# MoE routed in one level: experts ranked directly, slots gathered from the tokens, results added to x every turn, 18 ring slots in place of 16

## The reference, cut to what matters

```python
def hier_moe(h, w_rg, w_re, w_gate, w_up, w_down):
    pg_logits = h @ w_rg                       # 4 groups
    g_sel = argmax(pg_logits); p_sel = softmax(pg_logits)[g_sel]
    le_sel = (h @ w_re).reshape(..., 4, 8)[g_sel]   # the 8 experts of that group
    top_v, top_i = top_k(le_sel, 2)
    weights = p_sel * softmax(top_v)           # two experts per token
    expert_idx = g_sel * 8 + top_i             # of 32 experts
    act = silu(h @ w_gate[e]) * (h @ w_up[e]) * weights   # 1024 -> 256
    return act @ w_down[e]                     # 256 -> 1024, summed over the two experts
```

## Time and profile before

| | us |
|---|---|
| median of 3 runs (lowest to highest) | 1233.63 (1232.28 to 1236.47) |
| span of the profiled execution | 1228.4 |
| PE busy in the span | 1094.6 (89%) |
| DVE / ACT busy | 387.7 (32%) / 240.3 (20%) |
| moved by DMA | 298.75 MB, mean 243 GB/s |

### The profile page before, as it was taken

How to read it: one execution, slowest core, us unless ns; L and a number is a source line. 1 busy time by engine, 2 the same in 40 slices (tenths; PEclk the granted TensorE clock), 3 DMA queues, 4 the chain that set the end, 5 groups by cost and what they waited for, 6 DMA issues and landing times.

```text
span 1228.4 us, 15895 instructions
## 1 busy us (share of the span) xinstructions
PE 1094.6 (89%) x6152; PEld 601.8 (49%) x6152; DVE 387.7 (32%) x992; ACT 240.3 (20%) x494; POOL 86.3 (7%) x189
## 2 busy tenths in 40 slices
PE   8999988677799999998898799999999999879776
PEld 7776667364789446352333334444444634223232
DVE  2623354233683436211232120134001621123213
ACT  2320134232400113111111031131101311111102
POOL 6333130130000000000000000000000000000000
PEclk9999999898796999889989899999999998998889
DMA  9650374782700256699999994425423569999993
GB/s 296 175 174 12 99 246 134 205 338 87 267 1 1 77 154 257 283 421 421 421 421 420 419 305 152 132 78 205 146 103 138 239 249 421 423 421 420 420 420 123
DMA packets 87712, 298.75 MB, mean 243 GB/s; under 512 B 16067, under 2 KB 52475, under 8 KB 57902
## 3 DMA queue, kind: packets, MB, share of 16 engines
q1 hardware_dynamic: 73172, 273.92, 57.9%
q0 software_dynamic: 5152, 17.05, 4.6%
q10 hardware_dynamic: 9306, 6.67, 1.8%
HBM read 292.46 MB, written 5.16 MB: 242 GB/s over the span
## 4 chain that ended last, share of the span: by engine, by line
PE 76%; DMA 9%; DVE 7%; issue 3%; ACT 3%; SPq 2%; ACTq 0%; DVEq 0%
PE ps L1205 10%; PE ps L1395 9%; PE ps L760 9%; DMA arena<-in_moe_w_up 8%; PE ps L1161 5%; PE ps L1485 5%; PE ps L1232 3%; PE ps L711 3%; PE ps L720 2%; PE ps L1242 2%; PE ps L925 1%; PE ps L1388 1%; PE ps L1283 1%; PE ps L1012 1%; PE ps L991 1%
## 5 line engine op out<-in xcount | busy, mean ns | idle before, releaser
L1205 PE MATMUL ps<-arena,hT 128*32 128x512 f32 x1024 | 131.7, 658 | 23.0 <-DMA arena<-in_moe_w_up 22.4
L760 PE MATMUL ps<-hT,arena 128*128 128x288 f32 x448 | 114.1, 417 | 0.0
L1395 PE MATMUL ps<-arena,hT 128*128 128x512 f32 x256 | 112.7, 601 | 0.0
L760 PEld LDWEIGHTS ps<-hT,arena 128*128 128x128 f32 x448 | 86.5, 195 | 26.8 <-issue 1.7
L1205 PEld LDWEIGHTS ps<-arena,hT 128*32 128x32 f32 x1024 | 35.3, 119 | 106.5 <-issue 106.5
L1395 PEld LDWEIGHTS ps<-arena,hT 128*128 128x128 f32 x256 | 48.9, 192 | 60.8 <-issue 60.8
L1232 PE MATMUL ps<-arena 128*32 128x512 f32 x512 | 58.2, 595 | 3.2 <-ACT arena L1751 3.2
L1161 PE MATMUL ps<-htok,arena 128*128 128x512 f32 (+1 forms) x96 | 60.6, 765 | 0.0
L1485 PE MATMUL ps<-arena 128*128 128x512 f32 x128 | 59.2, 605 | 0.0
L2356 DVE TENSOR_TENSOR arena<-ps,lfp 128x256 f32<-128x256 f32 x16 | 6.8, 424 | 159.5 <-ACT lfp L1746 159.5
L711 PE MATMUL ps<-cum,ident 128*128 128x256 f32 x156 | 43.7, 439 | 11.8 <-issue 11.8
(11 more groups left out here) (473 smaller groups left out, 1446.1 us busy)
## 6 DMA issues: line engine op xcount, KB each, us to landing
arena<-in_moe_w_gate SPq DMA_DIRECT2D x66, 1024.0 KB, 14.5
arena<-in_moe_w_up SPq DMA_DIRECT2D x66, 1024.0 KB, 16.5
arena<-in_moe_w_down SPq DMA_DIRECT2D x66, 1024.0 KB, 21.7
arena<-in_cache_k SPq DMA_DIRECT2D x64, 256.0 KB, 3.2
arena<-in_cache_v POOLq DMA_DIRECT2D x64, 256.0 KB, 3.6
arena<-in_w_in_odd SPq DMA_DIRECT2D x16, 1024.0 KB, 10.5
arena<-in_w_in_even SPq DMA_DIRECT2D x14, 1024.0 KB, 9.3
arena<-in_w_out_odd SPq DMA_DIRECT2D x8, 1024.0 KB, 7.1
```

The lines of the kernel that those rows point to most:

```text
L760: last = mm(ps[:, c % 4, 0:T], w[:, k, P * (c % 2):P * (c % 2 + 1)], hT[:, k, :], start=k == 0, stop=k == KD - 1)
L1205: last = mm(ps[EC * j:EC * (j + 1), q % 2, :], xgT[:, k, GC * p + EC * j:GC * p + EC * (j + 1)], ring[:, sl:sl + 2, DE * k:DE * (k + 1)], ...
L1395: last = mm(ps[:, bank, :], hT[:, k, P * i:P * (i + 1)], ring[:, oslot(2 * n):oslot(2 * n) + 2, QC * k:QC * (k + 1)], start=k == 0, stop=k ...
```

## The change

The routing has one level. DVE finds both experts of a token, PE ranks all tokens per expert in one go (`ut`, `one` and a row `esr` that adds 512 times the expert's number, minus 1) and counts them. A token's place is thus one number, `sp1` or `sp2`. For every turn q, `places` compares `code` (the places of the turn's 128 slots) with `spq1`, `spq2` and gives `pl`, tokens x slots, and `gather` takes the 128 columns of slots straight from the token rows `htok` (8 steps k, three products of 128 columns each). `spread` copies `sp1`, `sp2`, `w1`, `w2` once per layer across all partitions (`spb`), from which `places_back` makes `pwT`, the weighted way back. `out_rows` adds a turn's results to x in every turn, one turn late. `pmg`, `hgt`, `ygs`, `group_sum`, `group_in`, `group_meta` and `group_rows` are gone. PSUM banks 5, 6, 7 serve gather and `out_rows` by turns, bank 2 the transposes. The spins before the first turn are 14 and 7 instead of 8, 4, 6 and 5. The ring has 18 slots; layer 1's mixer starts loading its first six units after the last `gate_up`, two more after the last `down` (before: four after the last but one `down`, four after the last). The overflow flag, the number of the hot expert and the rounds keep their meaning.

```diff
-ROUNDS = (TP + TS) // CH
-NPR = EG // QE
-NQ = NG * NPR
-PC = 4 * NG + 1
+ROUNDS = (TP + TS) // EC
+NQ = NE // QE
+PC = 2 * NQ + 1
-MSLOTS, RSLOTS = 3 * QE, 16
+MSLOTS, RSLOTS = 3 * QE, 18
-        arena = sb("arena", [P, SLOTS * UNIT + 23700])
+        arena = sb("arena", [P, RSLOTS * UNIT + 5240])
...
-                sp.wait_ge(s.dn_ps, past(0, r, NQ, NQ - (r == 0)))
-                for j in range(4):
+                sp.wait_ge(s.gu_ps, past(0, r, NQ, NQ))
+                for j in range(6):
                     odd_load(j)
                 sp.wait_ge(s.dn_ps, past(0, r, NQ, NQ))
-                for j in range(4, SLOTS):
+                for j in range(6, SLOTS):
...
-                spin(0, 8)
-                pe.wait_ge(s.rt_oh, 2 * layer + 1)
...
+                spin(0, 14)
+                pe.wait_ge(s.rt_oh, layer + 1)
+                for i in range(3):
+                    rk = ps[:, 4, NE * i:NE * (i + 1)]
+                    for j in range(i + 1):
+                        mm(rk, (ut if j == i else one)[0:n_, :], ohs[0:n_, j, :], start=j == 0, stop=False)
+                    mm(rk, one[0:1, :], esr[0:1, :], start=False, stop=True)
...
+                spin(0, 7)
+                    def gather(q, ks):
+                        for k in ks:
+                            if k == 0:
+                                W(s.p_rdy, NQ, q + 1)
+                                if q >= 2:
+                                    W(s.xadd, 5 * NQ, 5 * (q - 1))
+                                if first and q == 0:
+                                    pe.wait_ge(s.h_ready, rows_no(n) + 3)
+                            if k >= 3:
+                                W((s.xgd, s.xga)[(k - 3) % 2], 4 * NQ, 4 * q + (k - 3) // 2 + 1)
                             for i, (r0, m) in enumerate(TOK):
+                                last = mm(ps[:, row_bank(k), 0:P], htok[0:m, i, P * k:P * (k + 1)], pl[0:m, i, :],
                                           start=i == 0, stop=i == 2)
+                    def spread():
+                        pe.wait_ge(s.meta_rdy, layer + 1)
+                        for a, src in enumerate((sp1, sp2, w1, w2)):
+                            for i, (r0, m) in enumerate(TOK):
+                                last = mm(ps[:, (5, 6, 7, 2)[a], r0:r0 + m], bc(src[0:m, i, :], [m, P]), ident[0:m, 0:m],
+                                          start=True, stop=True)
+                            last.then_inc(s.spb_ps, 1)
+                        pe.wait_ge(s.spb_act, 2 * layer + 2)
+                        pe.wait_ge(s.spb_dve, 2 * layer + 2)
+                    def out_rows(q):
+                        W(s.y_ev, 2 * NQ, 2 * q + 2)
+                        W(s.pw_rdy, NQ, q + 1)
+                        if q:
+                            W(s.xadd, 5 * NQ, 5 * q)
                         for qr in range(4):
+                            last = mm(ps[TS * qr:TS * (qr + 1), row_bank(0), 0:QC], pwT[:, q % 2, TP:T],
+                                      ysb[:, QC * qr:QC * (qr + 1)], start=True, stop=True)
+                        for j in range(1, 5):
+                            if j >= 3:
+                                W(s.xadd, 5 * NQ, 5 * q + j - 2)
+                            mm(ps[:, row_bank(j), :], pwT[:, q % 2, P * i:P * (i + 1)], ysb[:, 512 * hf:512 * (hf + 1)],
+                               start=True, stop=True).then_inc(s.o_ps, 1)
...
                             gate_up(q, range(KD))
-                            group_sum(q - 1)
+                            out_rows(q - 1)
+                        elif first:
+                            spread()
                         act_turn(q)
-                        if p == 0 and g + 1 < NG:
-                            group_in(g + 1)
-                            group_rows(g + 1)
-                        if p == 1 and g + 1 < NG:
-                            slots_in(g + 1)
+                        if q + 1 < NQ:
+                            gather(q + 1, range(KD))
                         down(q)
-                        if p == 1 and 1 <= g < NG - 1:
-                            group_out(g - 1)
...
+                    def places(q):
+                        if q:
+                            W(s.g_ps, KD * NQ, KD * q)
+                        for i in range(3):
+                            last = V.tensor_scalar(pl[:, i, :], code[:, :], spq1[:, i, q:q + 1], None, ALU.is_equal)
...
+                    def places_back(q):
+                        V.scalar_tensor_tensor(pwT[:, q % 2, :], spb[:, 0, :], pcode[:, q:q + 1], spb[:, 2, :],
+                                               ALU.is_equal, ALU.mult)
...
+                        if q + 1 < NQ:
+                            places(q + 1)
+                        places_back(q)
                         W(s.silu, NQ, q + 1)
                         V.tensor_tensor(av[:, q % 2], ps[:, q % 2, DE:2 * DE], sg[:, q % 2], ALU.mult)
+                        if q:
+                            rows_out(q - 1)
+                        if q + 1 < NQ:
+                            rows_in(q + 1)
...
+                        places(0)
                         if first:
+                            weights()
+                        rows_in(0)
+                        if first:
+                            slots_of_turns()
...
+                            overflow()
```

More of the change, by code:

```diff
@@ L1171, in group_rows @@
[L1171 to L1188 removed]
+                            last.then_inc(s.g_ps, 1)
@@ L1234, in down @@
                         last.then_inc(s.dn_ps, 1)
-                    def group_sum(q):
-                        g, p = q // NPR, q % NPR
+                    def out_rows(q):
                         W(s.y_ev, 2 * NQ, 2 * q + 2)
-                        if p == 0 and g:
-                            W(s.yg_ev, 2 * NG, 2 * g)
-                        for hf in range(2):
-                            last = mm(ps[:, 5 + hf, :], pmwT[:, g % 2, p, :], ysb[:, 512 * hf:512 * (hf + 1)],
-                                      start=p == 0, stop=p == NPR - 1)
-                        last.then_inc(s.s1_ps, 1)
@@ L1356, in round_ @@
                         turn(NQ - 1)
-                        group_sum(NQ - 1)
-                        group_out(NG - 1)
+                        out_rows(NQ - 1)
                 round_(0, "turns")
```

524 lines of the change are left out of this document (180 added, 344 removed).

## The result

The changed kernel took 1251.58 us (median of 4 runs, 1247.99 to 1252.5), the kernel before 1235.05 us beside it (1232.28 to 1241.27): a ratio of 1.0135, 95% interval 1.0097 to 1.0173. Forecast were 1215 us and a range of 1202 to 1229. The sign was wrong, and the miss is 36.6 us.

A forecast was written before the change was run, and what follows sets the result against it. The prediction took each MoE layer as DMA-bound once its loads resume. Per layer -10.8 + 2.1 - 0.9 = -9.6 us, twice, plus 0.6, made -18.6: span 1209.8, launch 1215 us, range 1202 to 1229.

The forecast's parts named there:

- Step 1: Opening, up to the end of `gate_up` of turn 0: ends 11.2 us earlier, bounds 7 and 12.
- Step 2: Ring positions 16 and 17 load in the DMA hole, leaving 5.0 us less of loads after the resumption.
- Step 3: Turn 0 behind its `gate_up`: activation after 10.1 us, `down` done after 22.3, DMA standing still for 2.2.
- Steps 4 and 5: Turns 1 to 6: plain turn 21.4 us, another DMA stop of 3.2, `gate_up` 6 starts 170.8 after the resumption.
- Step 6: Turn 6 to the end: +2.1 us, then -0.9 from the last `gate_up`, and +0.6 once after layer 0.
- second stop: DMA waits for `gate_up` of turn 2, standing still another 3.2 us, bounds 0 and 8.
- The 12 us of cover: At turn 6 PE would be ready some 12 us before the data, after 158.7 us.
- the prediction's own sign of being wrong: The forecast is wrong if gather's products cost 0.3 us or more.
- the bound: Opening: with gather's products at 0.38 us each, eight steps are 4 us longer, so only 7 us earlier.
- rival C: Turns of 29 us, all in PE's chain: slower, 1284 us, deciding from 25.2 a turn; chance 0.10 in any size.
- B: PE partly replaces the DMA as bound, lower clock, turns of 25.4 us: 1223 to 1232 us; chance 0.18.

The follow-up runs named there:

- experiment 7: The changed kernel with the gather's sample-tile products reading 128 rows instead of 32, the added rows zero: 1223.82 us, ratio 0.9894.
- experiment 10: The changed kernel with the edits of experiment 7 and experiment 4, plus 128 rows in `spread` and the overfull expert's gather: 1208.63 us, ratio 0.9775.
- Experiment 3: The changed kernel with 16 ring slots instead of 18 and the earlier order of loads: 1257.94 us, ratio 1.0184.
- Experiment 6: The changed kernel with 2 spins instead of 7 behind the ranks: 1260.41 us, ratio 1.022.
- experiment 4: The changed kernel with DVE's `overflow` before the copies of `spb` and turn 0's activation before `places` and `places_back`: 1240.52 us, ratio 1.005.
- (8): The changed kernel with the edits of experiment 7 and experiment 4 together: 1211.07 us, ratio 0.981.

## Why the prediction was wrong, step by step

Layer 0 in three pieces, from the router's first transposes: up to the end of `gate_up` of turn 0 (the resumption), from there to the start of `gate_up` of turn 6, and from there to the gMLP's transposes.

| piece, us | before | forecast | measured | experiment 7 | experiment 10 |
|---|---|---|---|---|---|
| opening | 46.9 | 35.7 | 42.8 | 40.9 | 40.9 |
| to turn 6 | 170.5 | 170.8 | 183.0 | 173.9 | 166.0 |
| from turn 6 | 55.4 | 56.6 | 56.5 | 56.3 | 55.2 |
| sum | 272.8 | 263.1 | 282.2 | 271.1 | 262.0 |
| of it, DMA standing still in turns 0 to 2 | 0 | 5.4 | 15 | 7 | 0 |

**Step 1, the opening (forecast -11.2, measured -4.1).** Three terms were too small: ranks and counts 4.2 for 2.5, seven spins 5.7 for 3.3, and the stretch of gather and `gate_up` 16.1 for 12.8. The ranks' rows come apart by the clock: nine of the twelve products, up to 476.89 us, took 2.68 us at a granted clock of 1.00, 0.30 each, with rows of 128, 32 and 1 in turn; the last three took 1.56 us at 0.50. Half clock then lasted until 483.7, through most of the seven spins (0.54 on average). Experiment 3's layer 0 has the same opening at full clock, 39.6 us instead of 42.8. So about 3 us of the 7.1 that were missed are this fall of the clock, the rest is the price of the short products. The trace before had shown the fall too, in the spins that stood nearest, at a mean clock of 0.65:

```profile
479.29 4.24 PE L711 MATMUL ps<-cum,ident 128*128 128x256 f32 x12
```

Six spins, 0.7 each, where the prediction took 0.465 from the first eight. Experiment 6 shows that the seven pay for themselves all the same.

**Step 2, two slots (-5.0 a layer).** Right: experiment 3 lengthens the stretch that they act on by 4.9 and 6.3 us.

**Step 3, turn 0 (the step that failed, with step 4, by the price of gather).** The added wait was right: the activation began 10.2 us after `gate_up` and ended at 10.6 (10.1 forecast, though its terms as listed add up to 9.8). But `down` ended 30.5 us after the resumption, not 22.3. Of the 8.2 us, 7.1 are the gather, 14.89 for 7.8, and 0.9 `down`. The forecast's half-clock share was put down to PE's idle time; experiment 4 took most of that idle time away and kept 14.39 us. With 128 rows everywhere the same gather takes 7.92 (experiment 7), close to the forecast's number. So the changes of rows cost there too, and most of what looked like an effect of idling went with them. The stop of the DMA grew from the 2.2 us of the forecast to some 10: shares 0.19 and 0.84 from 520 to 540.

**Steps 4 and 5, the turns.** The forecast had a second stop of 3.2 us, PE free for turn 6 after 158.7 us and the data 12 us later, at 170.8. Measured: turn 6 starts after 183.0. Two delays ran side by side here.

- The stream. The second stop was some 5 us (share 0.45 over ten), both together 15 instead of 5.4. That is 10 of the 12.2 us by which the stretch was missed, and the last load for turn 6 landed 182.6 us after the resumption. These stops come from turns 0 to 2, where the gathers of turns 1 and 2 (8.2 us with `down`, and 3.4) held back the products that free the ring's slots.
- PE. It was free 24.3 us later than forecast, nearly all of it gather: 7.1 in turn 0, and 5 x 3.4 = 17.0 in turns 1 to 5. The 12 us of cover were named; they were less than half of what was needed.

Both ended together, in layer 0 within 0.4 us (in layer 1 the load landed at 1184.45 and PE started at 1185.02). So the prediction's model, a stream plus its stops, still accounts for the time; its stops were nearly three times too small, and its cover was used up as well. In experiments 7 and 10 the stretch shrinks with the stops: 15, 7 and 0 us of them go with 183.0, 173.9 and 166.0. A run that makes only the gathers of turns 3 on cheaper is not on record; by the landing time it would gain next to nothing.

**Step 6 (+1.2 in the table, measured +1.1).** Right as a sum, by luck: turn 6 itself was 4.0 us longer than before instead of 2.1, and the idle time at the branch 1.7 shorter (4.38 for 6.08), for which the runs show no reason.

**The term that was mis-sized** is thus one above all: 24 products at 0.213, taken from L694. That row has the same tiles of 128, 128 and 32 rows, and it showed no surplus. But it prints x3 for three transposes, one record each, while L1124 prints x12 for six products: a float32 product stands as two records. And the third transpose has 32 columns, not 128. In like weights its price holds (0.233 and 0.238), by luck: its records start 0.21 us apart, those of the two transposes in `act_turn`, of the same shape, 0.11. With the changes of rows it does not hold. Products of the right form with the changes stood in the trace before (a row of layer 1's chain, one of PE's timeline in layer 0):

```profile
971.87 0.90 PE ps L1128 x6
...
471.02 6.00 PE L1161 MATMUL ps<-htok,arena 128*128 128x512 f32 x12
```

L1128 is three products with tiles of 128, 128 and 32 rows, 0.30 each at full clock, which is the prediction's own sign of being wrong. In L1161 the records start 0.43 us apart in like rows and 0.52 to 0.53 around a change: 0.19 a change again. The 24 of `hot_in`, 0.38 each at a mean clock of 0.74, stood in the text as the bound, and rival C multiplied just that. They deserved more than a tenth.

**The rivals.** B came nearest: gather 7 (8.48), a turn of 25.4 (24.45), stops of 12 us (15), PE at turn 6 after 181 us (183.0). It said faster all the same, because it took over the opening's 11.2 us; with the measured 4.1 it ends on the other side. Rival C's point of decision rested on the same 11.2, and its own terms (7 x 21.4 grown by 22) give 24.5 us a turn and not 25.2; the measured turn stands just there. Two unsure terms that both lean to one side had been treated as if only one could fail.

**The skill's rule.** The Trainium skill, "TensorE: Matmul & The Clock Gate", Back-to-back issue gap, by its ratio of 1.45 made 7.4 us of a gather. The traces show 8.48 with changes of rows and 5.60 without: they do not bear out its ratio for like weights, and the changes of rows cost more than it says.

**What the change is worth.** With the price of gather as forecast (experiment 7) the launch took 1223.8 us, in the range but 9 above the forecast: what is left of the miss is in the opening (5.2 us in layer 0, 2 in layer 1) and in the stops of the DMA, 7 us in layer 0 instead of 5.4.

## What to carry to other kernels

Before a float32 product's price is taken from a row, compare its form: the records per instruction, the columns, the rows of the weights, and what rows its neighbours have. The start times of the records show a surplus that the mean of a row hides. A partial tile in a chain of short products was cheaper here read at full height over zeros than cut to its rows. Where the chain names one engine, look when the other bound was ready: here the last load landed 0.4 us before. And a helper's spins, or an engine's idle time, are judged by the clock of what follows, and by whether the engine stands still there anyway, so take them away in a run before counting them as a gain.

## What the runs showed of the hardware

- A change between weights of 128 and of 32 rows cost 0.19 us in a chain of two-record float32 products at full clock, with 128 columns (15 changes 2.88 us, 8 changes 1.54) and with 512 (L1161). With 32 columns it was 0.11 to 0.12, and from 32 rows to 1 none (0.11 us between records as in like rows, 476.58 us). The one-record transposes of L683 start 0.21 us apart in like rows and 0.21 into the tile of 32 rows. What in TensorE it is, was not settled.
- Fewer columns made such a product only a little cheaper and went with a lower clock: three quarters of the columns less in two of three products took 0.16 us off a step of 1.05, with a mean clock of 0.81 instead of 0.98 and a `down` of 5.77 us instead of 3.64.
- The stretch of half clock around turn 0's gather lasted 20.5 us in the changed kernel, 17.1 with most of the idle time gone (experiment 4), 10.2 with like rows in the gather (7), 6.8 with both (8) and 3.4 with like rows in `spread` too (10). So each took its part, the changes of rows the greatest. Why, is open.
